# Stage ends split two chunks at a time, additions ahead of slab remainders, and a reordered start in a two-block float32 network on one core

## Chip, cores and metric

The kernel runs on one core of one Trainium2 chip. The metric is the time of one execution in microseconds (us), the median over runs.

## What is computed

Two residual blocks over one sequence of 256 tokens and 1024 channels, all in float32. Each has two layers. What matters here is that every sublayer begins with an RMS norm and a projection of the normalised input, and ends with an addition to x:

```python
def first_block(x, ...):
    for layer in range(2):
        h = rms_norm(x, norm_mix[layer])
        x = x + hybrid_mixer(h, w_in[layer], ...)
        h = rms_norm(x, norm_ffn[layer])
        x = x + (swiglu(h, ...) if layer == 0 else moe_swiglu(h, ...))   # 8 experts, top 2
    return rms_norm(x, final_norm)

def second_block(x, ...):
    for l in range(2):
        h = swiglu_ffn(rmsnorm(x, ffn1_pre_g[l]), ...)
        x = x + 0.5 * rmsnorm(h, ffn1_post_g[l])
        h = mixing_sublayer(rmsnorm(x, mix_pre_g[l]), ...)   # gMLP, pool, sparse attention, convolution
        x = x + rmsnorm(h, mix_post_g[l])
        h = swiglu_ffn(rmsnorm(x, ffn2_pre_g[l]), ...)
        x = x + 0.5 * rmsnorm(h, ffn2_post_g[l])
    return x
```

In `mixing_sublayer` the convolution branch starts with `a * sigmoid(gt)`, the gated input; the sparse attention keeps the 64 best of each row of scores.

## The kernel before

**Weights come as slabs.** All large weights are one stream of slabs of 128 x 2048 floats (1 MB). SyncE loads each in two halves into one of six places (`Sync.slabs`, line 276 on; DMAs at line 286). Since float32 products are built from rounded parts, each slab is split: ScalarE copies each half to the rounded part `whi` (`Scalar.hi`, line 326; three places), VectorE subtracts to get the remainder `wlo` (`Vector.lo`, line 823). TensorE then takes three matmuls of 128 x 512 per chunk of 128 input channels (`term`, lines 1485 to 1487): whi with XH, wlo with XH, whi with XL. A slab is 24 matmuls. A place of `whi` is free again when TensorE has finished its slab (the semaphore `pe_slab`).

**Activations are split the same way.** X holds the residual as two tiles (t = 0, 1) of 128 tokens x 1024 channels. At the entry of a sublayer TensorE transposes a tile in eight chunks of 128 x 128 into PSUM (`norm_tile`, line 1552), ScalarE copies them to XH with the gain applied (`split_tile`, line 348), VectorE makes XL (`rest_tile`, line 853). The RMS factor comes later (`norm_in`: two squares at line 369, a square root at line 371, a reciprocal on VectorE at line 874) and is applied to the results.

**Every order is written out by hand,** one program per engine; each engine works its instructions in that order and waits at semaphores in front of them. There are ten such entries: m0.n, f0n, m1.n, e.n in the first block (two mixers, an FFN, the experts) and g10n, x0m.n, g20n, g11n, x1m.n, g21n in the second. `ENTRY` names for each what makes the tile ready, the first PSUM bank of tile 0 and of tile 1 (four chunks fill a bank, so a tile takes two banks), and the point in the matmuls at which tile 1 is transposed.

**A stage end.** The last two slabs of a sublayer are worked as a pair (`leave`, through `pair`), tile 0 with both slabs before tile 1; in the middle of the last quarter TensorE transposes tile 0 of the next sublayer. The next two slabs are a pair again (`enter`): tile 0 with both, then tile 1 with both. In the entries with a 4 tile 1 is transposed ahead of the second slab's first half, with an 8 ahead of the third quarter. The wide mixers of the second block (x0m, x1m) start with a slab of 256-column matmuls in which tile 0 needs all eight chunks at once. The waits of TensorE in `pair` are for both halves of `wlo` (`dve_lo`) and, once per quarter, for half of XL or all of it:

```python
if split:
    pe.wait_ge(*k.at(f"{split}.l{t}{1 if half == KT else s}"))
for i, term in enumerate(terms[t * half:(t + 1) * half]):
```

On VectorE `rest_tiles` is the same place: it finishes tile 0 of the sublayer before, makes XL of tile 0, then the `wlo` that is still owed (`self.owed`, one slab), then finishes tile 1 (`add`, line 882, or `post`, lines 1279 to 1286), then XL of tile 1. On ScalarE `norm_in` first loads the sqrt table by a dummy root (`root_table`, line 354) at the first four entries, then copies tile 0, one slab, tile 1.

**The start.** SyncE loads X in four DMAs, then slabs. GpSimd loads the per-channel columns (`pcols`), makes the identity, and loads constants of the first mixer (`mload`, `mask_load`: 768 and 448 KB) and the router's weights. ScalarE and VectorE split two slabs (`LEAD`) before the first entry.

**The lower bounds.** In the first block's mixers VectorE builds 16 diagonal tiles after the entry (`lower_bounds`, line 906), on which TensorE waits ahead of line 1581.

**Wide mixers on VectorE** (`Vector.mixer2`): index scores (SCO, lines 1373 and 1375), a slab's `wlo`, the gated input (line 1379, waits for group z3 of the projection), a top-k in eight rounds (line 1329 on; it needs the scores after GpSimd's selects, line 2122), 31 convolution taps (line 1349). TensorE transposes the gated input (line 1975) after two more slabs.

**The final norm of the first block** follows the experts. Behind them each engine reads a flag and branches past a second pass over the experts that is only taken when one overflows.

## Time and profile before

| | |
|---|---|
| runs (us) | 2960.80, 2957.74, 2963.33 |
| median | 2960.80 |
| the profiled execution | 2955.16, its span 2953.4 |
| mean granted TensorE clock | 0.986 of full |
| TensorE busy | 2833.4 us (96%) |
| VectorE busy | 2061.2 us (70%) |
| ScalarE busy | 1706.6 us (58%) |
| bytes moved | 633.65 MB, mean 215 GB/s |

Times in rows of the timeline count from the start of the span. A row has start, duration, engine, line, operation, out<-in with shapes, how many instructions it merges, and in brackets how long the engine was idle before and what ended that. PE is TensorE's matmuls, PEld its weight loads, DVE VectorE, ACT ScalarE, POOL GpSimd, SP SyncE. Matmuls are pipelined, so a matmul's duration is longer than the distance to the next one's start. "issue" means that the profile shows nothing that the engine waited for.

### The profile page before, as it was taken

The page shows a single profiled execution, that of the slowest core. Times are in us where ns is not written, and L with a number is a line of the kernel's source. Part 1 is how long each engine was busy: PE and PEld are TensorE (multiplying, and loading weights), DVE is VectorE, ACT ScalarE, POOL GpSimd, SP SyncE. Part 2 cuts the span into 40 slices and gives each one's busy share as a digit, 9 for nine tenths or more (in the row PEclk, how much of TensorE's full clock was granted, in tenths as well). Part 3 has the DMA queues.
Part 4 walks back from the last instruction along what each step waited for, and adds up shares of the span by engine and source line. Part 5 has one row for each costly group of instructions (what it writes and reads, how often), then busy time and mean ns, then how long its engine had stood idle before and what let it go on. Part 6 is the DMA issues. An engine that isn't in the chain of part 4 may idle for free.

```text
span 2953.4 us, 34430 instructions
## 1 busy us (share of the span) xinstructions
PE 2833.4 (96%) x13288; PEld 2340.7 (79%) x13288; DVE 2061.2 (70%) x2999; ACT 1706.6 (58%) x2373; POOL 32.6 (1%) x55
## 2 busy tenths in 40 slices
PE   7999999999998999999999989999899999888999
PEld 5888888788876888888888868777778788776787
DVE  5577655657767989888988955587665554787554
ACT  5555554555565777777777754455454544554543
POOL 0000000000001000000000000000000000000000
PEclk9999999999998999999999999999999999999999
DMA  6444455453356999999999955554455555444453
GB/s 217 157 134 135 160 194 186 161 171 129 129 194 225 362 354 356 347 346 359 351 344 352 358 179 185 179 171 143 145 187 183 190 185 187 163 151 148 164 185 114
DMA packets 173979, 633.65 MB, mean 215 GB/s; under 512 B 19584, under 2 KB 19584, under 8 KB 173808
## 3 DMA queue, kind: packets, MB, share of 16 engines
q1 hardware_dynamic: 171072, 621.88, 60.9%
q0 software_dynamic: 2736, 9.49, 0.9%
q8 instruction: 107, 1.75, 0.2%
q14 instruction: 64, 0.52, 0.1%
HBM read 629.20 MB, written 2.10 MB: 214 GB/s over the span
## 4 chain that ended last, share of the span: by engine, by line
PE 86%; DVE 8%; ACT 3%; issue 1%; DMA 1%; SPq 0%; DVEq 0%; ACTq 0%
PE ps L1485 26%; PE ps L1487 26%; PE ps L1486 26%; DVE wlo L823 3%; PE ps L1655 2%; DVE CA L1349 2%; PE ps L1739 1%; PE ps L1790 1%; ACT whi L326 1%; DVE XL L853 1%; DMA raw<-in_W 1%; ACT XH L348 1%; PE ps L1641 1%; PE ps L1642 1%; PE ps L1542 0%
## 5 line engine op out<-in xcount | busy, mean ns | idle before, releaser
L823 DVE TENSOR_TENSOR wlo<-raw,whi 128x1024 fp32r<-128x1024 f32 x1182 | 1386.0, 1221 | 453.5 <-ACT whi L326 447.0
L326 ACT ACTIVATE whi<-raw 128x1024 fp32r<-128x1024 f32 x1182 | 1187.9, 1058 | 495.9 <-PE ps L1487 488.1
L1485 PE MATMUL ps<-whi,XH 128*128 128x512 f32 (+1 forms) x2064 | 821.6, 398 | 52.6 <-DVE XL L853 39.7
L1487 PE MATMUL ps<-whi,XL 128*128 128x512 f32 (+1 forms) x2064 | 806.8, 391 | 0.0
L1486 PE MATMUL ps<-wlo,XH 128*128 128x512 f32 (+1 forms) x2064 | 806.8, 391 | 0.0
L1485 PEld LDWEIGHTS ps<-whi,XH 128*128 128x128 f32 x2064 | 392.3, 190 | 141.9 <-issue 24.6
L1487 PEld LDWEIGHTS ps<-whi,XL 128*128 128x128 f32 x2064 | 391.9, 190 | 82.4
L1486 PEld LDWEIGHTS ps<-wlo,XH 128*128 128x128 f32 x2064 | 392.7, 190 | 76.8 <-issue 0.5
L1485 PE MATMUL ps<-whi,XEH 128*128 128x512 f32 x704 | 280.9, 399 | 3.1 <-DVE wlo L823 1.7
L1487 PE MATMUL ps<-whi,XEL 128*128 128x512 f32 x704 | 275.2, 391 | 0.0
L1486 PE MATMUL ps<-wlo,XEH 128*128 128x512 f32 x704 | 274.1, 389 | 0.0
L1485 PE MATMUL ps<-whi,GH 128*128 128x512 f32 x440 | 172.6, 392 | 0.0
L1486 PE MATMUL ps<-wlo,GH 128*128 128x512 f32 x440 | 171.3, 389 | 0.0
L1487 PE MATMUL ps<-whi,GL 128*128 128x512 f32 x440 | 171.3, 389 | 0.0
L1485 PEld LDWEIGHTS ps<-whi,XEH 128*128 128x128 f32 x704 | 132.2, 188 | 30.0 <-issue 2.3
L1487 PEld LDWEIGHTS ps<-whi,XEL 128*128 128x128 f32 x704 | 132.1, 188 | 28.8
L1486 PEld LDWEIGHTS ps<-wlo,XEH 128*128 128x128 f32 x704 | 132.5, 188 | 25.8
L555 ACT ACTIVATE GH<-ps 128x512 fp32r<-128x512 f32 x55 | 33.0, 599 | 206.9 <-PE ps L1739 206.9
L1090 DVE TENSOR_TENSOR GL<-ps,GH 128x512 fp32r<-128x512 f32 x55 | 38.0, 692 | 162.3 <-ACT GH L555 162.3
L1485 PE MATMUL ps<-whi,GH_ 128*128 128x512 f32 x352 | 144.2, 410 | 0.0
L1487 PE MATMUL ps<-whi,GL_ 128*128 128x512 f32 x352 | 137.4, 390 | 0.0
L1486 PE MATMUL ps<-wlo,GH_ 128*128 128x512 f32 x352 | 137.3, 390 | 0.0
(365 smaller groups left out, 2648.4 us busy)
## 6 DMA issues: line engine op xcount, KB each, us to landing
raw<-in_W SPq DMA_DIRECT2D x1182, 512.0 KB, 4.9
GP<-in_ffn_post_g POOLq DMA_DIRECT2D x4, 512.0 KB, 4.0
X<-in_x SPq DMA_DIRECT2D x4, 256.0 KB, 3.9
skew<-RB POOLq DMA_DIRECT2D x4, 256.0 KB, 6.0
RB<-skew POOLq DMA_DIRECT2D x8, 128.0 KB, 6.6
GP<-in_mix_post_g POOLq DMA_DIRECT2D x2, 512.0 KB, 3.8
out<-X SPq DMA_DIRECT2D x2, 512.0 KB, 2.6
mload<-in_cum_sums POOLq DMA_DIRECT2D x1, 768.0 KB, 9.3
```

Source lines behind the costliest of these rows:

```text
L326: act.activation(k.whi[:, slot, part], k.raw[:, at, part], ACT.Copy).then_inc(*k.up("act_hi"))
L348: x = act.activation(k.XH[:, 4 * h + c, t * P:(t + 1) * P], k.ps[:, bank + h, c * P:(c + 1) * P], ACT.Copy, scale=gain(4 * h + c))
L555: act.activation(GH[:, 2 * g:2 * g + 2, :], src, ACT.Copy).then_inc(*k.up("act_split", f"{T}.gh{g}"))
L823: dve.tensor_tensor(k.wlo[:, at, part], k.raw[:, at, part], k.whi[:, slot, part], ALU.subtract).then_inc(*k.up("dve_lo"))
L853: x = dve.scalar_tensor_tensor(out=k.XL[:, j, t * P:(t + 1) * P], in0=k.ps[:, bank + h, c * P:(c + 1) * P], scalar=gain(j), in1=k.XH[:, j, ...
L1090: dve.tensor_tensor(GL[:, 2 * g:2 * g + 2, :], src, GH[:, 2 * g:2 * g + 2, :], ALU.subtract).then_inc(*k.up("dve_split", f"{T}.gl{g}"))
L1349: x = dve.scalar_tensor_tensor(out=CA[:, c, :], in0=HP[:, c, j:j + S], scalar=dw(c, j), in1=CA[:, c, :], op0=ALU.mult, op1=ALU.add)
L1485: pe.matmul(ps, xh, k.whi[:, slot, cols], start=first, stop=False)
L1486: pe.matmul(ps, xh, k.wlo[:, at, cols], start=False, stop=False)
L1487: return pe.matmul(ps, xl, k.whi[:, slot, cols], start=False, stop=last)
L1641: pe.matmul(k.ps[:, 4 + 2 * t + half, :], k.LFH[:, b, t, :], cols, start=True, stop=False)
L1655: mm = pe.matmul(o, x, x, start=True, stop=True)
```

## The change

- A tile's eight chunks go to four PSUM banks, two in each. `ENTRY` lists the banks of both tiles. TensorE signals every two chunks (`norm_tile`), ScalarE and VectorE wait and signal every two (`split_tile`, `rest_tile`), and TensorE waits for XL ahead of every second term in `pair`, in the router ahead of every second chunk. Tile 1's transposes wait for the last XL of tile 0.
- At f0n, m1.n and e.n VectorE finishes tile 1 (two additions) before the owed `wlo`, not after it.
- The dummy root at m0.n moves to the start of ScalarE's program. At f0n and m1.n it goes, so that the table load falls to the square root of line 371. At e.n it moves ahead of the last slab copy of the mixer before.
- Start: SyncE issues tile 0 of X, slab 0, tile 1, slab 1, and the rest. ScalarE and VectorE split one slab before the first entry, VectorE owes the next. GpSimd's constants wait until six half slabs have been copied.
- In the wide mixers VectorE's gated input moves up ahead of one slab's `wlo` and the scores.
- Final norm: ScalarE's first square waits for tile 0's last scatter addition, not for tile 1's.

```diff
-ENTRY = {"m0.n": ("x", 2, 6, 4), "f0n": ("m0.out", 4, 6, 4), "m1.n": ("f0.out", 2, 6, 4), "e.n": ("m1.out", 4, 6, 0), "g10n": ("fin.out", 2, 6, 8),
-         "x0m.n": ("g10p.out", 2, 6, 8), "g20n": ("x0m.p.out", 2, 4, 8), "g11n": ("g20p.out", 2, 6, 8),
-         "x1m.n": ("g11p.out", 2, 6, 8), "g21n": ("x1m.p.out", 2, 4, 8)}
+UP, OVER = (2, 3, 6, 7), (4, 5, 6, 7)
+ENTRY = {"m0.n": ("x", UP, UP, 4), "f0n": ("m0.out", OVER, OVER, 4), "m1.n": ("f0.out", UP, UP, 4), "e.n": ("m1.out", OVER, (4, 5, 0, 2), 0),
+         "g10n": ("fin.out", (0, 1, 2, 3), UP, 8), "x0m.n": ("g10p.out", UP, (3, 6, 7, 4), 8), "g20n": ("x0m.p.out", (0, 1, 2, 3), (2, 3, 4, 5), 8),
+         "g11n": ("g20p.out", UP, UP, 8), "x1m.n": ("g11p.out", UP, (3, 6, 7, 4), 8), "g21n": ("x1m.p.out", (0, 1, 2, 3), (2, 3, 4, 5), 8)}
...
                 sp.dma_start(k.X[:, t, part], k.a["x"][t * P:(t + 1) * P, part]).then_inc(*k.up(f"d_x{t}{h}", f"x{t}{h}", 16))
+            self.slabs(t + 1)
...
-        bank = ENTRY[tag][1 + t]
-        for h in range(2):
-            act.wait_ge(*k.at(f"{tag}.tp{t}{h}"))
-            for c in range(4):
...
+        banks = ENTRY[tag][1 + t]
+        for p in range(KT // 2):
+            act.wait_ge(*k.at(f"{tag}.tp{t}{p}"))
+            for c in (2 * p, 2 * p + 1):
+                x = act.activation(k.XH[:, c, t * P:(t + 1) * P], k.ps[:, banks[p], c % 2 * P:(c % 2 + 1) * P], ACT.Copy, scale=gain(c))
+            x.then_inc(*k.up("act_split", f"{tag}.h{t}{p}"))
...
-        if tag in ("m0.n", "f0n", "m1.n", "e.n"):
-            self.root_table()
         self.split_tile(tag, 0, gain)
...
-        self.early = 1
+        self.early = 0 if tag == "m0.n" else 1
...
-        self.hi(4)
+        self.hi(3)
+        if l:
+            self.root_table()
+        self.hi()
...
-        act.wait_ge(*k.at("x.end_dve"))
-        for t in range(NT):
+        for t in range(NT):
+            act.wait_ge(*k.at("x.end_dve" if t else "x.end_dve0"))
...
         act.wait_ge(*k.at("ones1"))
-        self.hi(LEAD)
+        self.root_table()
+        self.hi()
...
         self.rest_tile(tag, 0, gain)
+        added = tag in ("f0n", "m1.n", "e.n")
+        if added:
+            self.finish(1)
         self.lo(self.owed)
         self.owed = 0
-        if self.finish:
+        if self.finish and not added:
             self.finish(1)
...
         self.lo()
+        dve.wait_ge(*k.at(T + "z3"))
+        dve.tensor_tensor(A, A, GT, ALU.mult).then_inc(*k.up("dve_gate", T + "h"))
         self.lo()
         dve.wait_ge(*k.at(T + "rel"))
...
         self.lo()
-        dve.wait_ge(*k.at(T + "z3"))
-        dve.tensor_tensor(A, A, GT, ALU.mult).then_inc(*k.up("dve_gate", T + "h"))
...
-        self.lo(LEAD)
+        self.lo()
+        self.owed = 1
...
-                if split:
-                    pe.wait_ge(*k.at(f"{split}.l{t}{1 if half == KT else s}"))
                 for i, term in enumerate(terms[t * half:(t + 1) * half]):
                     if between and i:
                         between(8 * t + 4 * s + 4 * i / half)
+                    if split and i % 2 == 0:
+                        pe.wait_ge(*k.at(f"{split}.l{t}{i // 2 if half == KT else 2 * s + i // 2}"))
...
+        for p in range(KT // 2):
+            if p % 2 == 0:
+                pe.wait_ge(*k.at(f"{ready}{t}{p // 2}"))
+            if t and p == 0:
+                pe.wait_ge(*k.at(f"{tag}.l03"))
...
+        pool.wait_ge(k.of("act_hi"), 2 * RING)
         pool.dma_start(k.mload[:], k.a["cum_sums"]).then_inc(*k.up("d_mload", "mload", 16))
```

The order of instructions at three places. First ScalarE at the start, before (ACTIVATE whi is half a slab, XH one chunk, `small` the dummy root, later the RMS square root):

```order
L326 ACT_TABLE_LOAD
L326 ACTIVATE whi<-raw 128x1024 x4
L354 ACT_TABLE_LOAD
L354 ACTIVATE small<-small 128x1
L348 ACTIVATE XH<-ps,pcols 128x128 x8
L326 ACTIVATE whi<-raw 128x1024 x2
L348 ACTIVATE XH<-ps,pcols 128x128 x8
L369 ACTIVATE XN,small<-X 128x1024 x2
```

and now:

```order
L356 ACT_TABLE_LOAD
L356 ACTIVATE small<-small 128x1
L328 ACTIVATE whi<-raw 128x1024 x2
L350 ACTIVATE XH<-ps,pcols 128x128 x8
L328 ACTIVATE whi<-raw 128x1024 x2
L350 ACTIVATE XH<-ps,pcols 128x128 x8
L369 ACTIVATE XN,small<-X 128x1024 x2
L371 ACTIVATE small<-small 128x2
```

One slab's two halves stand ahead of the first XH instead of two slabs', and the table load of the root stands ahead of everything.

VectorE at f0n, before (XL one chunk, `wlo` half a slab, X<-ps an addition of 512 columns):

```order
L882 TENSOR_TENSOR X<-ps,X 128x512 x2
L853 SCALAR_TENSOR_TENSOR XL<-ps,pcols,XH 128x128 x8
L823 TENSOR_TENSOR wlo<-raw,whi 128x1024 x2
L882 TENSOR_TENSOR X<-ps,X 128x512 x2
L853 SCALAR_TENSOR_TENSOR XL<-ps,pcols,XH 128x128 x8
L874 RECIPROCAL small<-small 128x2
```

and now:

```order
L888 TENSOR_TENSOR X<-ps,X 128x512 x2
L856 SCALAR_TENSOR_TENSOR XL<-ps,pcols,XH 128x128 x8
L888 TENSOR_TENSOR X<-ps,X 128x512 x2
L827 TENSOR_TENSOR wlo<-raw,whi 128x1024 x2
L856 SCALAR_TENSOR_TENSOR XL<-ps,pcols,XH 128x128 x8
L880 RECIPROCAL small<-small 128x2
```

The additions of tile 1 and the owed half slabs have changed places; m1.n and e.n read alike.

VectorE in a wide mixer, before (Z<-Z is the gated input, SCO the index scores, WRK the top-k's copy):

```order
L1366 TENSOR_SCALAR small<-small 128x8
L823 TENSOR_TENSOR wlo<-raw,whi 128x1024 x4
L1373 TENSOR_SCALAR SCO<-XN,small 128x256 x2
L1375 SCALAR_TENSOR_TENSOR SCO<-XN,small,SCO 128x256 x6
L823 TENSOR_TENSOR wlo<-raw,whi 128x1024 x2
L1379 TENSOR_TENSOR Z<-Z 128x2x256
L1380 MEMSET HP 128x2x30
L1329 COPY WRK<-SCO 128x512
```

and now:

```order
L1373 TENSOR_SCALAR small<-small 128x8
L827 TENSOR_TENSOR wlo<-raw,whi 128x1024 x2
L1376 TENSOR_TENSOR Z<-Z 128x2x256
L827 TENSOR_TENSOR wlo<-raw,whi 128x1024 x2
L1382 TENSOR_SCALAR SCO<-XN,small 128x256 x2
L1384 SCALAR_TENSOR_TENSOR SCO<-XN,small,SCO 128x256 x6
L827 TENSOR_TENSOR wlo<-raw,whi 128x1024 x2
L1387 MEMSET HP 128x2x30
```

The gated input has moved ahead of two half slabs and of the eight score instructions.

## Rows read from the trace of the kernel before

**Rows 1.** The page: busy us, share of the span, instructions of each engine.
```profile
PE 2833.4 (96%) x13288; PEld 2340.7 (79%) x13288; DVE 2061.2 (70%) x2999; ACT 1706.6 (58%) x2373; POOL 32.6 (1%) x55
```
**Rows 2.** What TensorE waited for: us in total, times, longest.
```profile
PE ps L1485 <- DVE XL L853: 39.7, 15, 13.9
...
PE ps L1975 <- DVE Z L1379: 5.7, 2, 2.9
```
**Rows 3.** Timeline of TensorE at three entries: x0m.n (twice) and g21n.
```profile
1910.16 0.35 PE L1485 MATMUL ps<-whi,XH 128*128 128x256 f32 x1 [1.79 <-DVE XL L853]
...
1919.88 0.38 PE L1485 MATMUL ps<-whi,XH 128*128 128x256 f32 x1 [2.99 <-DVE XL L853]
...
2766.41 0.50 PE L1485 MATMUL ps<-whi,XH 128*128 128x512 f32 x1 [1.96 <-DVE XL L853]
```
**Rows 4.** Timeline of the start.
```profile
12.84 1.06 ACT L326 ACTIVATE whi<-raw 128x1024 fp32r<-128x1024 f32 x1 [0.78 <-DMA raw<-in_W]
...
21.44 0.76 PE L1485 MATMUL ps<-whi,XH 128*128 128x512 f32 x1 [13.91 <-DVE XL L853]
```
**Rows 5.** Windows of the start: stretch, length, busy us (count), PEclk, DMA share, GB/s.
```profile
0.00:5.00 5.00, 0.00 (x0) 0.00 (x0) 0.22 (x2) 0.00 (x0) 3.46 (x11) 1.00 0.59 184
5.00:8.00 3.00, 1.97 (x8) 1.57 (x8) 0.00 (x0) 0.00 (x0) 0.73 (x3) 1.00 1.00 245
8.00:21.00 13.00, 0.00 (x0) 0.00 (x0) 5.74 (x8) 8.89 (x15) 0.00 (x0) 1.00 1.02 399
```
**Rows 6.** Timeline of the stage end f0n.
```profile
354.26 1.28 ACT L354 ACT_TABLE_LOAD   x1
...
355.19 0.39 PE L1486 MATMUL ps<-wlo,CVH 128*128 128x512 f32 x1
355.42 0.39 PE L1487 MATMUL ps<-whi,CVL 128*128 128x512 f32 x1
...
355.67 2.17 ACT L348 ACTIVATE XH<-ps,pcols 128x128 fp32r<-128x128 f32 x8
356.83 2.16 DVE L853 SCALAR_TENSOR_TENSOR XL<-ps,pcols,XH 128x128 fp32r<-128x128 f32 x8 [6.03 <-ACT XH L348]
...
358.10 0.47 PE L1485 MATMUL ps<-whi,XH 128*128 128x512 f32 x1 [2.29 <-DVE XL L853]
...
358.91 2.35 DVE L823 TENSOR_TENSOR wlo<-raw,whi 128x1024 fp32r<-128x1024 f32 x2
...
361.18 1.28 DVE L882 TENSOR_TENSOR X<-ps,X 128x512 f32<-128x512 f32 x2
...
362.52 1.03 PE L1552 MATMUL ps<-ident,X 128*128 128x128 f32 x8
```
**Rows 7.** Timeline behind the experts, ScalarE and VectorE.
```profile
1708.60 1.28 ACT L354 ACT_TABLE_LOAD   x1 [4.89 <-issue]
...
1713.06 0.16 DVE L1263 RECIPROCAL small<-small 128x1 f32<-128x1 f32 x1 [4.39 <-ACT small L647]
```
**Rows 8.** Timeline of the first wide mixer, VectorE and GpSimd.
```profile
1937.64 2.36 DVE L823 TENSOR_TENSOR wlo<-raw,whi 128x1024 fp32r<-128x1024 f32 x2 [7.32 <-ACT whi L326]
...
1943.43 2.70 POOL L2122 TENSOR_SCALAR_AFFINE_SELECT SCO<-SCO 128x256 f32<-128x256 f32 x2 [27.46 <-DVE SCO L1375]
...
1946.78 0.43 DVE L1329 COPY WRK<-SCO 128x512 f32<-128x512 f32 x1
...
1963.51 2.36 DVE L823 TENSOR_TENSOR wlo<-raw,whi 128x1024 fp32r<-128x1024 f32 x2 [0.95 <-ACT whi L326]
```
**Rows 9.** Windows behind four waits, columns as in rows 5.
```profile
358.80:362.20 3.40, 3.40 (x10) 2.65 (x9) 3.40 (x5) 0.92 (x1) 0.00 (x0) 0.50 0.41 167
884.50:894.60 10.10, 4.71 (x22) 3.44 (x23) 6.46 (x16) 6.71 (x16) 0.54 (x1) 0.50 0.33 125
1919.90:1923.30 3.40, 3.40 (x26) 3.33 (x27) 2.20 (x3) 1.38 (x4) 0.00 (x0) 1.00 0.00 0
2522.80:2526.20 3.40, 3.40 (x19) 3.40 (x18) 3.33 (x6) 1.37 (x2) 0.00 (x0) 0.50 0.61 222
```

More of the change, by code:

```diff
@@ L847, in rest_tile @@
         dve, k = self.eng, self.k
-        bank = ENTRY[tag][1 + t]
-        for h in range(2):
-            dve.wait_ge(*k.at(f"{tag}.h{t}{h}"))
-            for c in range(4):
-                j = 4 * h + c
-                x = dve.scalar_tensor_tensor(out=k.XL[:, j, t * P:(t + 1) * P], in0=k.ps[:, bank + h, c * P:(c + 1) * P], scalar=gain(j),
-                                             in1=k.XH[:, j, t * P:(t + 1) * P], op0=ALU.mult, op1=ALU.subtract)
-            x.then_inc(*k.up("dve_split", f"{tag}.l{t}{h}"))
+        banks = ENTRY[tag][1 + t]
+        for p in range(KT // 2):
+            dve.wait_ge(*k.at(f"{tag}.h{t}{p}"))
+            for c in (2 * p, 2 * p + 1):
+                x = dve.scalar_tensor_tensor(out=k.XL[:, c, t * P:(t + 1) * P], in0=k.ps[:, banks[p], c % 2 * P:(c % 2 + 1) * P], scalar=gain(c),
+                                             in1=k.XH[:, c, t * P:(t + 1) * P], op0=ALU.mult, op1=ALU.subtract)
+            x.then_inc(*k.up("dve_split", f"{tag}.l{t}{p}"))
     def rest_tiles(self, tag, gain):
@@ L1166, in experts @@
             self.scatter(T, NE - 1, t)
+        k.events[f"{T}.end_dve0"] = k.events[f"{T}.add{NE - 1}.0"]
         k.events[f"{T}.end_dve"] = k.events[f"{T}.add{NE - 1}.1"]
@@ L1547, in norm_tile @@
         pe, k = self.eng, self.k
-        ready, bank = ENTRY[tag][0], ENTRY[tag][1 + t]
-        for h in range(2):
-            pe.wait_ge(*k.at(f"{ready}{t}{h}"))
-            for c in range(4):
-                mm = pe.transpose(k.ps[:, bank + h, c * P:(c + 1) * P], k.X[:, t, (4 * h + c) * P:(4 * h + c + 1) * P], k.ident[:])
-            mm.then_inc(*k.up("pe_turn", f"{tag}.tp{t}{h}"))
+        ready, banks = ENTRY[tag][0], ENTRY[tag][1 + t]
+        for p in range(KT // 2):
+            if p % 2 == 0:
+                pe.wait_ge(*k.at(f"{ready}{t}{p // 2}"))
+            if t and p == 0:
+                pe.wait_ge(*k.at(f"{tag}.l03"))
+            for c in (2 * p, 2 * p + 1):
+                mm = pe.transpose(k.ps[:, banks[p], c % 2 * P:(c % 2 + 1) * P], k.X[:, t, c * P:(c + 1) * P], k.ident[:])
+            mm.then_inc(*k.up("pe_turn", f"{tag}.tp{t}{p}"))
     def enter(self, tag, first, second, events):
```

12 lines of the change are left out of this document (5 added, 7 removed).

## The prediction

> **What bounds the kernel now.** I read the page first: TensorE is busy for 96% of the span [rows 1], so outside a few places nothing else can be worth time, and the 120 us in which it is idle are all there is to win, with what its clock loses. Next comes the list of what TensorE waits for: the remainders XL of the normalised input (line 853), 39.7 us in 15 waits, and the gated input Z (line 1379), 5.7 us in 2 [rows 2]. Then the timeline of one stage end, step by step [rows 6], and of the start [rows 4], to see which engine holds TensorE there; the other ends repeat the pattern [rows 3]. What the reader is to see is that at a stage end three engines work in a row: TensorE transposes, ScalarE copies (XH), VectorE subtracts (XL), and TensorE stands still until the first piece has gone through all three. The size of that piece is what the change halves or quarters.
>
> **Pieces and pace.** Eight transposes take 1.03 us, so 0.13 each; eight copies 2.17, so 0.27 each; eight remainders 2.16, so 0.27 each [rows 6]. A piece of four chunks becomes one of two: a wait that contains the whole chain shrinks by two of each, 0.26 + 0.54 + 0.54 = 1.34 us. Later pieces need not be feared: six matmuls of 512 columns follow per pair of chunks (0.23 us each from start to start, 355.19 to 355.42 [rows 6]), 1.36 us, against 0.54 for the next pair on ScalarE and VectorE.
>
> **1. Start.** TensorE begins at 21.44, after 13.91 us of idleness, and the second half of the first slab has landed only at 12.84 [rows 4]. Bytes moved: 184 GB/s for 5 us, 245 for 3, then 399 [rows 5]; at 12.84 that is 3.6 MB (an estimate), though input and first slab are 2.1 MB: the constants (1.25 MB) were in between. Now pcols, half the input and the slab come first, 1.62 MB, which the same rates have moved at 7.9; the second half of the input and the second slab are then there at 11.9. The sqrt table is loaded while nothing waits for it. Working on: copy of the half slab 1.06 to 9.0, its remainder 1.2 to 10.2, two XL 0.6, start at 10.9. The second slab's remainder (behind XL on VectorE, copies of 1.06 each behind XH on ScalarE) ends near 14.9; TensorE has then done four chunks of the first slab and eight transposes if it runs at full clock (14.7), and is not yet there (16) at the lower one, which its first matmul had (0.76 against 0.39). Gain about **10.8**. The first lower-bound chain starts as much earlier. ScalarE now has two slabs to copy behind it instead of one, 2 us; what hides them is that it waits for TensorE itself a little later, and without that cover the third group of matmuls would come up to 2 us later. The constants start with the sixth copied half slab near 23 and are needed after the first six groups, near 100 us: nothing. Bounds: if later slabs share the bandwidth with the first, it may land near 10.3 (gain 8.4); at most 12.
>
> **2. Second token tile, where it was waited for in full.** At the four FFN entries of the second block the wait is 1.96 [rows 3] (the last of four alike) and becomes 0.6: 4 x 1.34 = 5.4, less 0.05 each for two more signals: 5.2. At the two wide mixers the first matmuls wait for all eight chunks, 2.99 [rows 3]; now two fewer copies, six fewer remainders and two fewer transposes stand in the way: 0.54 + 1.62 + 0.26 = 2.42 each; I take 4.7. Together **9.9**.
>
> **3. First token tile of the second block.** The copies end 1.1 us sooner for the first pair, but the second slab's remainder is queued on VectorE behind all eight XL, and TensorE needs it after four chunks. That is the wait that comes next. The XL end only some 0.5 earlier. At the three FFN entries behind a mixer or an FFN this leaves 0.45 each. At the wide mixers idle is 1.79 [rows 3]; TensorE then does 24 short matmuls (3.0 us) while the remainder takes 2.35, so 0.8 were in hand and the gain is 0.5 + 0.8 = 1.25 each. At the first entry of the second block nothing is owed, but VectorE finishes tile 1 first; between 0.45 and 1.1 I take 0.7. Together **4.5**.
>
> **4. f0n and m1.n.** The pair before ends at 355.81; the table load keeps XH back to 355.67, and the matmuls start at 358.10 [rows 6]. Without the load (1.28 and 0.15 around it) XH starts at 354.3, XL at 354.9, and the first two are there at 355.6: no wait. Then the next waiting: four chunks to 358.6, the additions (now straight after XL, 357.2 to 358.5) let the transposes run to 359.6, and the remainder moved behind the additions ends at 358.5 + 2.35 = 360.8. TensorE waits 1.2 us and goes on at 360.9; before, it got there at 363.3, after a stretch in which matmuls took 0.63 from start to end. Gain 2.4. The load isn't gone: it now comes before the Sqrt (line 371). In f0n TensorE covers it. In m1.n it stands in the chain to the lower bounds, on which TensorE also waits, but the chain starts earlier by that same load and by the additions: again 2.4. Together **4.8**. The Trainium skill (ScalarE: Activation LUTs, section What ACT_TABLE_LOAD costs) states some 1.38 us of drain beside a load of 1.28; here the first copy follows 0.13 us after the load's end, with the dummy root in between [rows 6], so the trace doesn't agree. By the skill's figure m1.n would gain 1.0 and the sum be 1.4 less.
>
> **5. e.n.** Here the load is issued earlier, in an idle stretch, and tile 1 can't be turned before its addition, which stood behind the load (1.43) and the slab remainder (2.35) [rows 6]. Both go from its way: **3.8**. The router behind it is a chain of small steps and moves as a whole.
>
> **6. Gated input in the wide mixers.** TensorE waits 2.85 us twice. VectorE's product now goes into its idle time of 7.32 [rows 8]: ScalarE finishes group z3 ahead of the copies for which VectorE is idle there. So the wait goes. But from there to the channel sum VectorE is the limit, and TensorE merely arrives sooner at its next waits for remainders. What counts is how much sooner VectorE is: not by the whole product, since its next step waits for GpSimd, whose two selects end at 1943.43 + 2.70 = 1946.13 against 1946.78 [rows 8]: 0.6; and in the first mixer its waits for copied slabs fall too, 0.95 at 1963.51 [rows 8] and a smaller one before it, together 1.5. **2.7** in all for both. Bounds: 1.2 (no such wait falls) and 5.7 (both waits of TensorE go in full).
>
> **7. Final norm.** Split flags let the first square start before the second addition. ScalarE's table load begins at 1708.60 with nothing to wait for but the branch before it, and VectorE's reciprocal at 1713.06, long after its input [rows 7]. The branch sets both: **0**.
>
> **8. Clock.** Behind some of these waits the granted clock is 0.50, that is 1.2 of 2.4 GHz: 3.4 us at 358.8, and again in the second wide mixer at 2522.8 [rows 9]. At half the clock such a stretch does the work of 1.7 us, so it costs up to 1.7. In 4 this is contained. For the entry of the second wide mixer I add **1.4**, short of 1.7 because a wait lay in it as well.
>
> **Sum.** 10.8 + 9.9 + 4.5 + 4.8 + 3.8 + 2.7 + 0 + 1.4 = 37.9 us, against the profiled execution's 2955.2 (span 2953.4): 2917.3. That execution stands 5.6 below the median of the runs shown, 2960.8, so for a median I forecast **2922.9**. What a measurement here can tell from no change is 0.2%, 5.9 us.
>
> **Rivals.** *The clock doesn't follow* (0.12). What stays is not nothing: 1.2 at f0n and m1.n, 0.6 at six waits for tile 1. For it: 2.29 us of idleness before 358.10 led to a slow stretch [rows 6, 9], and 1.2 is not far below. Against it: behind 2.99 at 1919.88 [rows 3] the clock stayed full [rows 9]. Then 4.2 of the gains in 4 and 8 fall away, and four ends that had no stretch get one, 6.8: gain 27, **2934**. *The slabs aren't sooner* (0.10): if the first slab lands at 12.84 as before, because bandwidth and not order holds it, TensorE starts at 15.8, gain 5.6 in place of 10.8: **2928**. Against it: 3.6 MB had been moved by then. *More comes back* (0.05): slow stretches of 10 us at e.n [rows 9] and at the first entry of the second block shorten by a third each and the mixers' upper bound holds: gain 44, **2917**. *Slower* (0.03): where TensorE was stopped once it now may be stopped four times, from bank to bank, and each stop may keep the clock low. At e.n the trace shows what this costs: 0.50 for 10.1 us [rows 9], 5.1 lost. Two more such stretches at each of ten ends are 101 us, less 38: **3024**; from 3.8 us lost per end on the change is no gain. Against it: while a pair's next pieces come in 0.54 and are used in 1.36 no stops arise. The Trainium skill has such a case (TensorE: Matmul & The Clock Gate, section A second HAM failure mode: psum-queue depth-cycling): short idle times while going round the banks make the clock swing. By that rule this rival would come true; no row here shows stops of that kind. *Nothing measurable* (0.02): gains at the ends and the start each swallowed by an unseen wait, 2960.
>
> **Numbers.** The forecast has 0.68. Lower gain: start -2.4, clock -4.2, mixers -1.5, so 30; upper 43 (start +1.2, mixers +3, and one slow stretch less). With 2.5 us for the spread of the runs shown this is 2915 to 2934, and the first rival's time, itself uncertain by 1, takes it to 2935; outside lie the slow rival and no change, 0.05, and the tails of the others. Faster 0.95 (all but the last two), same 0.02, slower 0.03.
>
> **What would show it.** Right: TensorE's first 512-column matmul near 11 (wrong if after 14); waits for XL down from 39.7 to about 5 us beyond the start's share, new ones for the slab remainder (line 827) of 1.2 at f0n and m1.n; no wait for line 1376, but longer ones for remainders and for the channel sum before 2011; 1708.60 and the table load there merely shifted. Wrong: ten or more waits per end; slow stretches behind each; VectorE idle between the top-k and the channel sum.

## The result, and the profile after

| | before | changed |
|---|---|---|
| median of the runs | 2959.27 (2956.76 to 2963.33, 4 runs) | 2924.86 (2917.68 to 2925.10, 4 runs) |
| ratio | | 0.9876, 95% interval 0.9861 to 0.989 |
| the profiled execution, its span, granted clock | 2955.16, 2953.4, 0.986 | 2924.62, 2922.9, 0.988 |
| the changed kernel once more, as a control (e9) | 2959.04 (7 runs) | 2916.91 (2916.17 to 2917.00, 4 runs), ratio 0.9856 (0.984 to 0.9873); span 2915.1, granted clock 0.990 |

The change is faster, by 34.4 us in one measurement and 42.1 in the other; the forecast was 37.9. The same program was measured at two times 8 us apart; e9 below shows where they differ. A "slow stretch" is one in which the granted clock is recorded as 0.50 [rows 9]. The page after, to be read against [rows 1]:

```profile
PE 2835.2 (97%) x13288; PEld 2341.1 (80%) x13288; DVE 2060.9 (71%) x2999; ACT 1702.8 (58%) x2370; POOL 36.9 (1%) x55
```

TensorE's busy time hasn't fallen, although no matmul was added and 30.5 us went: what fell is its idle time, from 120.0 to 87.7. What it waited for after, in us, times and longest:

```profile
PE ps L1493 <- DVE wlo L827: 17.1, 17, 2.0
PE ps L1550 <- DVE XN L1447: 13.9, 2, 6.9
PE ps L1493 <- DVE XL L856: 8.8, 8, 3.8
PE ps L1563 <- DMA pcols<-in_pcols: 7.5, 1, 7.5
PE ps L1928 <- DVE CA L1356: 5.7, 2, 2.8
PE ps L1563 <- DVE X L1275: 5.4, 1, 5.4
```

The remainders XL fell from 39.7 in 15 waits [rows 2] to 8.8 in 8, 3.8 of it at the start, so 5.0 elsewhere, as forecast; the wait for Z is gone. Slab remainders (wlo) are now the largest item. Where the time went shows best as distances between the same events in three traces, beside the sum of the prediction's terms for each stretch. "Tile 1 at" an entry is the first matmul of the second token tile there; the channel sum is L1928 (L1917 before):

| stretch, from the event above to | before | changed | changed, e9 | forecast gain | gain, gain e9 |
|---|---|---|---|---|---|
| lower bounds of the first mixer | 36.70 | 29.98 | 29.64 | 10.8 (term 1) | 6.7, 7.1 |
| lower bounds of the second (f0n, m1.n between) | 528.05 | 520.47 | 520.47 | 4.8 (4) | 7.6, 7.6 |
| the router's sums, L1884 (e.n between) | 334.55 | 332.18 | 330.50 | 3.8 (5) | 2.4, 4.1 |
| tile 1 at g10n | 828.33 | 827.03 | 827.15 | 2.0 (2, 3) | 1.3, 1.2 |
| tile 1 at x0m.n | 192.25 | 189.14 | 189.10 | 3.6 (2, 3) | 3.1, 3.2 |
| channel sum of the first wide mixer | 91.84 | 89.80 | 89.81 | 2.1 (6) | 2.0, 2.0 |
| tile 1 at g20n | 137.46 | 139.37 | 137.19 | 1.8 (2, 3) | -1.9, 0.3 |
| tile 1 at g11n | 190.54 | 189.15 | 189.12 | 1.8 (2, 3) | 1.4, 1.4 |
| tile 1 at x1m.n | 193.75 | 189.10 | 189.14 | 5.0 (2, 3, 8) | 4.7, 4.6 |
| channel sum of the second wide mixer | 91.67 | 89.84 | 89.82 | 0.6 (6) | 1.8, 1.9 |
| tile 1 at g21n | 141.27 | 139.47 | 135.80 | 1.8 (2, 3) | 1.8, 5.5 |
| end of the span | 186.99 | 187.37 | 187.36 | 0 | -0.4, -0.4 |
| sum | 2953.4 | 2922.9 | 2915.1 | 38 | 30.5, 38.3 |

**The start after.** Rows of ScalarE, VectorE and TensorE, then windows with the columns of [rows 5]:

```profile
9.05 1.06 ACT L328 ACTIVATE whi<-raw 128x1024 fp32r<-128x1024 f32 x1 [6.75 <-DMA raw<-in_W]
10.29 1.06 ACT L328 ACTIVATE whi<-raw 128x1024 fp32r<-128x1024 f32 x1 [0.19 <-DMA raw<-in_W]
...
10.14 2.47 DVE L827 TENSOR_TENSOR wlo<-raw,whi 128x1024 fp32r<-128x1024 f32 x2 [9.03 <-ACT whi L328]
12.53 2.15 DVE L856 SCALAR_TENSOR_TENSOR XL<-ps,pcols,XH 128x128 fp32r<-128x128 f32 x8
...
13.28 0.77 PE L1493 MATMUL ps<-whi,XH 128*128 128x512 f32 x1 [3.80 <-DVE XL L856]
...
18.54 1.23 PE L1563 MATMUL ps<-ident,X 128*128 128x128 f32 x8
```

```profile
0.00:5.00 5.00, 0.00 (x0) 0.00 (x0) 0.22 (x2) 1.49 (x2) 1.38 (x7) 1.00 0.51 142
5.00:8.00 3.00, 0.49 (x3) 0.49 (x4) 0.00 (x0) 0.00 (x0) 0.00 (x0) 1.00 0.91 291
...
13.30:18.50 5.20, 5.20 (x12) 3.99 (x13) 3.65 (x8) 2.00 (x3) 0.00 (x0) 1.00 1.03 418
```

The slab's second half is there at 10.29, not at 7.9. By 8.0 the queues had moved 142 x 5 + 291 x 3, so 1.6 MB, as much as everything up to the slab's end holds; but it wasn't those 1.6 MB alone: from 2.67 on SyncE had issued the transfers behind them, and by 10.29 2.38 MB had moved. The bound written down was landing 10.3, gain 8.4; this trace has 10.29 and, for the first matmul, 8.2 (21.44 to 13.28). How exactly that fits is partly luck. Eight traces have this start unedited (the changed kernel, e3, e4, e5, e7, e9, e10, e12), and in them ScalarE's copy of the second half begins at 9.20 to 10.29, the first matmul at 12.18 (e3) to 13.28, the first lower bounds at 28.50 to 29.98. Against the one trace of before the gain is thus 8.2 to 9.3 at the first matmul and 6.7 to 8.2 at the lower bounds. In this trace another 1.2 goes to TensorE's pace: all twelve matmuls ahead of the transposes (13.28 to 18.54) follow each other by some 0.43, in the kernel before only the first six, and then by 0.23; in the other seven it is seven to twelve.

**f0n after**, VectorE and TensorE, in place of [rows 6]:

```profile
346.35 2.16 DVE L856 SCALAR_TENSOR_TENSOR XL<-ps,pcols,XH 128x128 fp32r<-128x128 f32 x8 [3.98 <-ACT XH L350]
348.43 1.28 DVE L888 TENSOR_TENSOR X<-ps,X 128x512 f32<-128x512 f32 x2
349.62 2.35 DVE L827 TENSOR_TENSOR wlo<-raw,whi 128x1024 fp32r<-128x1024 f32 x2
...
349.96 1.03 PE L1563 MATMUL ps<-ident,X 128*128 128x128 f32 x8
352.03 0.50 PE L1493 MATMUL ps<-whi,XH 128*128 128x512 f32 x1 [1.03 <-DVE wlo L827]
```

As forecast: no wait for XL, tile 1 turned without one, and a new wait of 1.03 (1.2 expected) for the slab remainder behind the additions.

### The profile page after: what moved, and what is told of

It is laid out like the page before. It is cut to its first block, busy times and chain, and to the rows that moved or that the text cites. A ratio compares the mean times of both kernels' runs of the same rounds, so it can differ in the third digit from the quotient of the medians.

```text
span 2922.9 us, 34438 instructions
## 1 busy us (share of the span) xinstructions
PE 2835.2 (97%) x13288; PEld 2341.1 (80%) x13288; DVE 2060.9 (71%) x2999; ACT 1702.8 (58%) x2370; POOL 36.9 (1%) x55
## 4 chain that ended last, share of the span: by engine, by line
PE 86%; DVE 9%; ACT 3%; issue 1%; DMA 1%; POOL 0%; SPq 0%; DVEq 0%; ACTq 0%; POOLq 0%
PE ps L1493 26%; PE ps L1495 26%; PE ps L1494 26%; DVE wlo L827 3%; PE ps L1666 2%; DVE CA L1356 2%; PE ps L1750 1%; PE ps L1801 1%; ACT whi L328 1%; DVE XL L856 1%; DMA raw<-in_W 1%; PE ps L1652 1%; PE ps L1653 1%; PE ps L1550 0%; DVE Z L1443 0%
```

## Experiments

Twelve kernels ran, e1 to e8 on one chip and e9 to e12 on another, each with runs of the kernel before beside it. Their medians are compared with the control's 2916.9, since those runs agree within 1 us; the medians of before beside the three sets of runs are 2958.7, 2961.8 and 2959.0, so a difference below about 3 is read from the trace and not from the medians.

**e1, pieces of four chunks.** The table ENTRY and the loops of split_tile, rest_tile, norm_tile, pair and the router's waits as before, everything else changed:

```diff
-        for p in range(KT // 2):
-            act.wait_ge(*k.at(f"{tag}.tp{t}{p}"))
-            for c in (2 * p, 2 * p + 1):
+        for h in range(2):
+            act.wait_ge(*k.at(f"{tag}.tp{t}{h}"))
+            for c in range(4):
```

> The changed kernel with pieces of four chunks again at the stage ends (banks, copies, remainders, transposes and their signals as before); start, order of the additions, table load, gated input and final norm stay changed. Theory (the pieces carry about half the gain): tile-1 waits of the second block back from 0.70 to 1.96 four times and to 2.99 twice, 9.6 us; the first tile there 4.5; f0n and m1.n 0.75 each; start 1.1; clock 1.4: 18 us slower than the change, 2943. Rival 1 (the gain is in the order of the additions and the start, the pieces only fill time that the slab remainder sets anyway): tile 1 alone, 9.6: 2934.5. Rival 2 (going round four banks costs clock): no slower than the change, 2925 or less.

Measured: 2941.18 (2936.24 to 2948.04), 24 slower than the control. In its trace the waits for XL are back:

```profile
PE ps L1493 <- DVE XL L856: 26.8, 15, 4.0
```

From the last experts' scatter on, the six entries are 0.9, 3.1, 2.1, 1.4, 4.6 and 1.6 longer than in e9, 13.8 in all before rounding (14.1 plus 1.4 of clock expected); f0n and m1.n cost 1.7 once the clock is counted out (1.5 expected). Another 3 us are slow stretches in the second wide mixer. Theory held, both rivals fell: the pieces carry about half the gain, and if going round four banks costs anything, it is less than they bring (the two were not separated).

**e2, the start of before.**

```diff
-            self.slabs(t + 1)
...
-        self.root_table()
-        self.hi()
+        self.hi(LEAD)
...
-        pool.wait_ge(k.of("act_hi"), 2 * RING)
```

> The changed kernel with the start of before: all input and then slabs, mixer constants at once, two slabs copied ahead of the first stage end, table load there. Theory (from the trace after: first 512-column matmul 13.28 against 21.44, of which the smaller pieces give 1.1): first matmul at about 20.3, and 7 us slower, 2932. Rival 1 (the forecast's price, 10.8 less 1.1): 2934.6. Rival 2 (the first lower-bound chain swallows most of an earlier start): the shift seen at the first slab gone by the end of the first mixer's groups, under 3 us slower, 2927.

Measured: 2923.25, 6.3 slower than the control; first matmul at 21.24 and the first lower bounds at 37.59 against 29.64 to 29.98 in the two traces of the changed kernel, 7.6 to 8.0 later. The whole shift survives the first mixer (f0n's second slab 7.6 later). In the whole span 2.3 of it are made up by places that weren't edited, 1.4 of them behind the first channel sum, where e9 has a slow stretch and e2 none. The theory held but for its 20.3. The first matmul comes 0.2 sooner than before although the slab's second half landed 0.7 later (13.53 against 12.84): from the first copy of the input to the matmul it is 1.40 in place of 2.43, so the pieces bring their 1.0.

**e6 and e11, the parts of the start.** One kernel loads the constants at once, the other issues the whole input before the first slab:

```diff
-        pool.wait_ge(k.of("act_hi"), 2 * RING)
```

> The changed kernel with the mixer constants and masks loaded at once instead of behind the sixth copied half slab; the order of input and slabs stays changed. Theory (1.25 MB more share the bandwidth before the first slab is complete): first 512-column matmul 2 to 3 us later than 13.28, near 15.7. Rival (the order of SyncE's transfers did it, the constants run beside them): first matmul within 0.7 of 13.28.

```diff
-            self.slabs(t + 1)
```

> The changed kernel with all four pieces of the input ahead of the first slab on SyncE, constants still late and one slab copied ahead of the stage end. Theory (the gain at the start is that one slab and not two is copied and subtracted before the first piece of the input, 2.1 and 2.4 us, and that half the input is 0.5 MB less in front): first 512-column matmul 1 to 1.5 later than 13.3, near 14.5. Rival (the order of transfers is the whole gain): near 17 or later.

Measured: 2915.98 and 2917.97. TensorE's first matmul in e6:

```profile
13.07 0.77 PE L1493 MATMUL ps<-whi,XH 128*128 128x512 f32 x1 [3.35 <-DVE XL L856]
19.86 0.50 PE L1493 MATMUL ps<-whi,XH 128*128 128x512 f32 x1 [1.01 <-DVE wlo L827]
```

It is at 13.07 there, at 13.32 in e11, at 12.18 to 13.28 with the changed start. Neither edit alone shows beyond that scatter (e6's second slab is late by a wait of 1.01, which the next wait, for the lower bounds, takes up), so the constants theory (15.7) fell and e11's (14.5) too. Only in e2, where both are undone, does the second half land at 13.53 in place of 9.20 to 10.29. What is left is the rest of the chain: with two slabs ahead the input's copies follow at 19.84, behind the second slab (to 18.42) and a table load of 1.28.

**e3, additions behind the slab remainder.**

```diff
-        added = tag in ("f0n", "m1.n", "e.n")
+        added = False
```

> The changed kernel with tile 1's addition behind the owed slab remainder on VectorE at f0n, m1.n and e.n, as before. Theory: e.n 2.35 later; at f0n and m1.n the wait for the remainder (1.0) goes but the transposes of tile 1 wait for the additions 2.25 instead, 1.2 later each: 4.8 us slower, 2929.7. Rival (at f0n and m1.n the two orders trade one wait for an equal one): 2.4 slower, 2927.3, with the difference at e.n alone.

Measured: 2917.95, 1.0 slower. At f0n the wait moves from the slab remainder (1.03) to the transposes (1.32), and from tile 0's first transpose to the matmul behind tile 1's transposes it is 7.48 in place of 7.06, so 0.4; at m1.n the same, and the lower bounds behind it wait 2.98 in place of 1.83. At e.n:

```profile
869.37 2.35 DVE L827 TENSOR_TENSOR wlo<-raw,whi 128x1024 fp32r<-128x1024 f32 x2
871.64 1.28 DVE L888 TENSOR_TENSOR X<-ps,X 128x512 f32<-128x512 f32 x2
873.77 2.16 DVE L856 SCALAR_TENSOR_TENSOR XL<-ps,pcols,XH 128x128 fp32r<-128x128 f32 x8 [0.84 <-ACT XH L350]
```

and in the changed kernel:

```profile
868.54 2.16 DVE L856 SCALAR_TENSOR_TENSOR XL<-ps,pcols,XH 128x128 fp32r<-128x128 f32 x8 [3.98 <-ACT XH L350]
870.61 1.28 DVE L888 TENSOR_TENSOR X<-ps,X 128x512 f32<-128x512 f32 x2
871.81 2.35 DVE L827 TENSOR_TENSOR wlo<-raw,whi 128x1024 fp32r<-128x1024 f32 x2
874.07 2.16 DVE L856 SCALAR_TENSOR_TENSOR XL<-ps,pcols,XH 128x128 fp32r<-128x128 f32 x8
...
871.35 1.47 PE L1563 MATMUL ps<-ident,X 128*128 128x128 f32 x8 [1.79 <-DVE X L888]
874.83 0.37 PE L1873 MATMUL ps<-XH,RWS 128*16 128x256 f32 x1 [2.01 <-DVE XL L856]
```

The same work of VectorE stands between the two XL in either order. From the first XL to the second it is 6.47 in e3 and 5.53 in the changed kernel: 0.9, and not 2.35; from the end of the pair before (869.17 + 0.39 in the changed kernel) to the router's sums (L1884) 13.59 against 13.07 and 13.12, 0.5. The total of some 2.4 (0.4 at f0n, 1.5 at m1.n with its lower bounds, 0.5 at e.n) is the rival's, but for another reason: most of it is at m1.n, not at e.n. The medians alone, 1.0 apart, can't tell this.

**e4, the table ahead of the copies.**

```diff
+        if tag in ("f0n", "m1.n", "e.n"):
+            self.root_table()
         self.split_tile(tag, 0, gain)
...
-        self.hi(3)
-        if l:
-            self.root_table()
-        self.hi()
+        self.hi(4)
```

> The changed kernel with the sqrt table loaded ahead of the copies at f0n, m1.n and e.n, as before. Theory (a load costs 1.28 and 0.15 around it, no drain): XH 1.4 later at each, TensorE's first wait at f0n and m1.n 1.2 later at each, e.n 1.4: 3.8 us slower, 2928.7. Rival 1 (each load drains the engine for 1.38 more before the next copy): XH 2.8 later at each, 7.5 slower, 2932.4. Rival 2 (in m1.n the load stands in the chain to the lower bounds in either place, at f0n the remainder sets the wait anyway): e.n alone, 1.4 slower, 2926.3.

Measured: 2918.78, 1.9 slower. f0n in e4, ScalarE and TensorE:

```profile
346.65 1.28 ACT L356 ACT_TABLE_LOAD   x1
347.95 0.20 ACT L356 ACTIVATE small<-small 128x1 f32<-128x1 f32 x1
348.06 2.16 ACT L350 ACTIVATE XH<-ps,pcols 128x128 fp32r<-128x128 f32 x8
...
349.45 0.47 PE L1492 MATMUL ps<-whi,XH 128*128 128x512 f32 x1 [1.25 <-DVE XL L855]
```

The added wait is 1.25 at f0n and 1.23 at m1.n (1.2 each expected), and by the distance used in e3 each costs 1.5 (8.59 against 7.06); but at m1.n the lower bounds, with the load no longer in their chain, then wait 0.55 in place of 1.83: 1.3 is given back. At e.n it is 14.36 from the pair's end to the router's sums in place of 13.1, 1.3 more. Together about 3.0, between the theory and rival 2. Rival 1 fell: from the end of the load to the first copy it is 0.13, with the root in between.

**e5, the gated input behind again.**

```diff
-        dve.wait_ge(*k.at(T + "z3"))
-        dve.tensor_tensor(A, A, GT, ALU.mult).then_inc(*k.up("dve_gate", T + "h"))
         self.lo()
         dve.wait_ge(*k.at(T + "rel"))
...
         self.lo()
+        dve.wait_ge(*k.at(T + "z3"))
+        dve.tensor_tensor(A, A, GT, ALU.mult).then_inc(*k.up("dve_gate", T + "h"))
         dve.memset(HP[:, :, 0:30], 0.0)
```

> The changed kernel with the product for the gated input behind the scores and a slab remainder again, in both wide mixers, as before. Theory (VectorE is the limit up to the channel sum): TensorE waits 2.85 for Z twice, its waits for remainders before the channel sum are shorter, and from the first matmul of tile 1 to the channel sum the stretch is 91.8 in the first and 91.7 in the second mixer, as before, in place of 89.8: 3.9 us slower in these two stretches. Rival 1 (the forecast's terms): 2.1 in the first, 0.6 in the second. Rival 2 (each wait of 2.85 counts in full): 5.7. The time of the whole is this plus or minus 7, which slow stretches of TensorE's clock add or take: 2922 to 2929.

Measured: 2918.76 (2915.74 to 2922.09), 1.9 slower. From tile 1 to the channel sum 90.60 and 90.35, against 89.80 and 89.84: 1.3 in both mixers together, below all three expectations, although both waits of 2.84 for Z are back. So the moved product alone isn't what shortened 91.84 to 89.80. The rest is in the clock behind the wait for Z, and in what VectorE then waits for. In the kernel before, first mixer:

```profile
1946.00:1952.80 6.80, 6.07 (x17) 4.92 (x18) 6.59 (x17) 2.49 (x3) 0.14 (x1) 0.50 0.31 114
1956.92 2.36 DVE L823 TENSOR_TENSOR wlo<-raw,whi 128x1024 fp32r<-128x1024 f32 x2 [0.62 <-ACT whi L326]
```

and in e5, first mixer (a window, a row) and second (a window):

```profile
1926.30:1929.70 3.40, 3.40 (x10) 2.62 (x9) 3.26 (x13) 2.30 (x3) 0.00 (x0) 0.50 0.21 87
1940.95 2.36 DVE L827 TENSOR_TENSOR wlo<-raw,whi 128x1024 fp32r<-128x1024 f32 x2 [0.28 <-ACT whi L328]
2532.20:2539.00 6.80, 6.78 (x32) 5.70 (x33) 6.59 (x18) 3.11 (x4) 0.00 (x0) 1.00 0.27 100
```

The releasers in the traces read thus: a slow stretch behind the wait for Z delays TensorE's slab, ScalarE's next copy waits for that slab, and VectorE for the copy. With 6.8 us of it VectorE waits 0.62 and 0.95 [rows 8], with 3.4 us 0.28, with none not at all, and the distances are 91.84, 90.60 and 90.35. The second mixer of before has none there either; its 91.67 is 90.35 and a slow stretch at 2533.0, just as tile 1 begins, which costs 1.3 (VectorE's first wait for a copied slab ends 6.93 behind tile 1's first matmul, 5.61 in the first mixer). So the move itself is worth 0.5 in each mixer (90.35 to 89.82), and the rest of 91.84 and 91.67 is the clock's, not the pieces'. The wait for Z comes with such a stretch in two of its four cases (before and e5, first mixer each).

**e7 and e10, a shift.** Eight or sixteen more transposes ahead of those of g10n, into a bank that the real ones overwrite, and nothing else:

```diff
+            if tag == "g10n" and t == p == 0:
+                for _ in range(8):
+                    pe.transpose(k.ps[:, banks[0], 0:P], k.X[:, 0, 0:P], k.ident[:])
```

> The changed kernel with eight more transposes (1.03 us of TensorE, their result overwritten) ahead of the first at g10n, and nothing else. Theory (which waits in the wide mixers are followed by a slow stretch depends on when they fall, not on what the change did there): the stretches behind 1988 and 2063 and their two fellows in the second mixer come or go although nothing there was edited; the time is 1.03 longer plus or minus 1.7 for each stretch, 2918 to 2926, and not 2925.9. Rival (the longer waits that the earlier product leaves before the channel sum cause them): the same stretches, each 1.0 later, and 2925.9.

> The changed kernel with sixteen more transposes (2.06 us of TensorE) ahead of the first at g10n. Theory (stretches depend on when waits fall): the time doesn't follow the shift; between 2916 and 2927, with another set of slow stretches behind 1695 than with eight. Rival (only the first small shift cured something): one more us than with eight, 2918.3, and the same stretches.

Measured: 2917.30 (2916.63 to 2917.67, 5 runs) with eight, 2918.31 (2917.23 to 2923.72) with sixteen. The kernel with more work is 7.5 faster than the first measurement of the changed kernel. In the second wide mixer, which isn't touched, the changed kernel (first trace) has these stretches behind the channel sum and behind the wait for XL at L1434:

```profile
2596.00:2599.40 3.40, 3.34 (x11) 2.88 (x12) 3.33 (x6) 0.00 (x0) 0.00 (x0) 0.50 0.48 192
2671.10:2674.50 3.40, 3.40 (x10) 2.62 (x9) 2.83 (x3) 1.39 (x2) 0.00 (x0) 0.50 0.00 0
```

and e7, at the same events:

```profile
2592.40:2595.80 3.40, 3.39 (x19) 2.98 (x20) 3.37 (x5) 1.47 (x4) 0.00 (x0) 1.00 0.83 295
2667.50:2670.90 3.40, 3.40 (x17) 2.82 (x16) 1.82 (x3) 0.58 (x1) 0.00 (x0) 1.00 0.00 0
```

At the lower level (0.50, 1.2 of 2.4 GHz) TensorE starts 10 and 11 instructions in 3.4 us, at the full one 17 and 19. With sixteen neither is there either, and the stretch behind the first mixer's channel sum, which with eight still stands at 1987.9, is gone too. e7's rival fell. That of e10 had the time right (2918.3) and only the stretches wrong. The theory isn't shown by this: the unedited program differs from its first measurement in the same way (e9), so these two runs can't tell what a shift does from what comes and goes by itself.

**e9, the control.** No edit.

> The changed kernel itself, unedited, as a control beside the others. Theory (its time is the sum of its waits plus slow stretches that come or go from run to run and with small shifts): runs fall into a group near 2917 and one near 2925, with granted clocks of 0.991 and 0.987. Rival (the slow stretches belong to this schedule, which has the additions ahead, the table late and the earlier product all at once): all runs within 1.5 of 2925.

Measured: 2916.91, all four runs within 0.9, clocks 0.990 to 0.991. So the theory's two groups don't lie within this set but between it and the first (2924.62, 2925.10 and 2925.10 at 0.987 and 0.988, and 2917.68 at 0.991); the rival fell. The chip may differ between the two sets; one run of the first set at the other time says that it isn't needed. The second wide mixer in the first trace:

```profile
2587.49 0.50 PE L1493 MATMUL ps<-whi,XH 128*128 128x512 f32 x1 [1.98 <-DVE wlo L827]
2596.06 2.08 PE L1928 MATMUL ps<-CA,ones 128*128 128x256 f32 x4 [2.83 <-DVE CA L1356]
...
2669.82 0.50 PE L1493 MATMUL ps<-whi,XH 128*128 128x512 f32 x1 [1.93 <-DVE XL L1434]
```

and in e9:

```profile
2583.38 0.50 PE L1493 MATMUL ps<-whi,XH 128*128 128x512 f32 x1 [1.96 <-DVE wlo L827]
2591.94 1.13 PE L1928 MATMUL ps<-CA,ones 128*128 128x256 f32 x4 [1.22 <-DVE CA L1356]
...
2664.09 0.50 PE L1493 MATMUL ps<-whi,XH 128*128 128x512 f32 x1 [1.93 <-DVE XL L1434]
```

One program, and it reads thus. The channel sum comes 8.57 and 8.56 behind the wait before it in both, because VectorE sets it. In e9 a slow stretch (2584.4 to 2587.8) lies inside that time and costs nothing: TensorE merely arrives later and waits 1.22 in place of 2.83. In the first trace the stretch lies behind the channel sum, where TensorE is the limit: four matmuls take 2.08 in place of 1.13, and it is 73.76 to L1434 in place of 72.15; behind L1434 another 1.7 go the same way. In all fourteen traces the distance from a channel sum to L1434 is either 72.1 to 72.2 or 73.7 to 73.8, whatever was edited: 73.7 or more in eight of 28 cases, all behind a channel sum that TensorE waited 2.81 to 2.83 for, and 72.1 to 72.2 in the eighteen behind a wait of some 1.2 (and in two, in e3 and e8, behind 2.8). Of the 7.8 between the two spans 3.7 are behind this channel sum, 2.2 behind the first mixer's, 1.7 behind the second lower bounds and 0.3 at the start (table above). What starts a slow stretch in one execution and not in the other stays open.

**e12, the final norm's flags together.**

```diff
-        for t in range(NT):
-            act.wait_ge(*k.at("x.end_dve" if t else "x.end_dve0"))
+        act.wait_ge(*k.at("x.end_dve"))
+        for t in range(NT):
```

> The changed kernel with the final norm's first square behind both additions again. Theory (the branch before it sets the start): from the last scatter's first matmul to the first transpose of g10n 8.86 as in the changed kernel, with 0.3 either way. Rival (the square comes one addition sooner): 0.7 longer, 9.5.

Measured: 2915.33 (2912.17 to 2916.70), not slower; from the scatter to the transposes 9.70, but the other kernels, whose norm is the changed one, spread from 8.71 to 9.97 here. Not told apart, and worth nothing in the time.

**e8, a version that goes further.**

```diff
-                    pe.wait_ge(k.of("dve_lo"), 2 * (self.n - 2 + s) + 2)
+                    pe.wait_ge(k.of("dve_lo"), 2 * (self.n - 2 + s) + (1 if by_half else 2))
...
+                    if t == 0 and by_half and i == 2:
+                        pe.wait_ge(k.of("dve_lo"), 2 * (self.n - 2 + s) + 2)
```

In ENTRY the last number of the six entries of the second block is 7 in place of 8; at m0.n the first slab's copies and remainders stand between the second and third piece of the input's.

> The changed kernel with three additions. At the stage ends TensorE waits for the owed slab's remainder half by half (its first two chunks need the first half only); in the second block tile 1 is turned one chunk earlier; at the start the first slab's copies and remainders come between the first and second half of the input's. Theory: the waits for the remainder at f0n and m1.n (1.0 each) and the six of 0.6 in the second block go, 5.9; six waits of 0.70 for tile 1 go, 4.2; first matmul 1.5 to 2 sooner than 13.28: 12 us faster but for the clock, 2913 plus or minus 7. Rival (VectorE is as late with what comes next: the waits move behind, to tile 1's additions and copies): 3 us, 2922.

Measured: 2911.90 (2910.66 to 2917.16, 5 runs), ratio to before 0.983 (0.9816 to 0.9843), the fastest of all; 5.0 below the control's median. First matmul at 11.86 (11.3 to 11.8 expected; the changed start scatters from 12.18 to 13.28); the waits for slab remainders at the entries and for tile 1 are gone. But:

```profile
PE ps L1495 <- DVE wlo L828: 13.9, 10, 2.2
...
PE ps L1568 <- DVE X L1296: 3.5, 5, 0.8
```

Tile 1 is now waited for one step earlier, at its addition: 3.5 of the 4.2 come back. At m1.n the wait for the lower bounds grows from 1.83 to 2.98, so 1.1 comes back there too. The 5.0 lie between the rival's 3 and the theory's 12, for the rival's reason.

## Why the prediction was right, and where not

The direction and the mechanism were right, and the size was within the range: 37.9 us forecast, 30.5 and 38.3 in the two traces, 34.4 and 42.1 in the medians. That e9's 38.3 agrees so well with 37.9 is partly luck: terms 1 to 7 were forecast at 36.5 and come to some 32 (an estimate: 7, 12.4, 5.9, 4.1 and 2.6 from the items below), and slow stretches that the trace of before has and e9 hasn't make up the rest. By terms:

1. **Start, 10.8: mis-sized.** 8.2 at the first matmul, 6.7 to 7.1 at the lower bounds (9.3 and 8.2 in the best of the eight traces). The failed step is "which the same rates have moved at 7.9": the rates came true (1.6 MB by 8.0), but it gave the first slab the whole bandwidth. Of the sum only the bound named beside it (10.3) came. That "the constants were in between" as the cause is only half right: with either the constants' delay or the order alone the slab lands about as early (copied from 10.34 in e11, 10.09 in e6).
2. and 3. **Tile 1, 9.9, and tile 0, 4.5: right in kind, 2 us too large, and that in tile 0.** Tile 1's wait is 0.70 at all six entries (0.6 forecast), so 4 x 1.26 + 2 x 2.29 = 9.6 of 9.9; tile 0's next wait is for the slab remainder, 0.57 to 0.72. With slow stretches counted at half their length the six entries give 12.4 of 14.4, which leaves tile 0 some 2.8 of 4.5. e1 shows the same from the other side.
4. **f0n and m1.n, 4.8: 7.6 in the table,** of which 1.7 is a slow stretch at 37.9 in the trace of before. Neither trace of the changed kernel has one there, but e10, the same program up to g10n, has one at 30.1. That leaves 5.9: by the distance used in e3 2.85 at each entry (9.91 to 7.06; 2.4 forecast), and 0.2 at the lower bounds. The waits are as forecast. Taken back one at a time, the additions are worth 1.9 here (e3), the table 1.7 (e4), the pieces 1.7 (e1), together 5.3 of the 5.9. The table's is what is left of 3.1, since at m1.n the wait for the lower bounds gives 1.3 back.
5. **e.n, 3.8: right in sum, wrong in its parts.** From the end of the pair before to the router's sums it was 17.1 and is 13.1 in both traces, 4.1. (The table's 2.4 in the first trace has a slow stretch of 1.7 at the lower bounds in it, 551.4 to 554.8.) But "both go from its way" fails for the slab remainder: it moved from before the addition to before the next XL, and the router needs both tiles' XL. Alone the addition's place gives 0.5 (e3), the table 1.3 (e4), the pieces, which the term left out, 0.8 (e1: 13.89); the other 1.5 comes only with all three. Up to the first of the router's matmuls (L1873), with less of the slow stretches in it, it is 9.70 before and 5.27 in both traces of the changed kernel, and 6.20 (e3), 6.78 (e4) and 6.29 (e1): 0.9, 1.5 and 1.0 of 4.4, with 1.0 left. Where that comes from is not shown.
6. **Gated input, 2.7: 3.9 in the stretches, 1.3 by taking the move back (e5).** The parts are nearly the forecast's: 0.5 in each mixer for the product (0.6 forecast), and in the first VectorE's waits for copied slabs gone (0.62 and 0.95; 1.5 forecast). What the term didn't have is why those waits were there, a slow stretch behind the wait for Z, and the 1.3 of another at 2533.0 (e5). "TensorE merely arrives sooner at its next waits" was right: the waits before the channel sum are 7.7 in the first mixer before (2.85 for Z, 1.68, 1.98, 1.19) and 8.2 after (0.88, 1.96, 0.51, 1.99, 2.83).
7. **Final norm, 0: right.** The table load starts 3.51 behind the scatter, as before (3.52), with its 4.89 of "issue" ahead of it [rows 7].
8. **Clock, 1.4: right at x1m.n (4.7 in the table against 3.1 at x0m.n), wrong as the whole account.** The prediction reckoned with what the clock does at the places that change, not with stretches that come and go elsewhere. Behind the two channel sums they took some 3.5 each in the first trace (139.37 and 139.47, against 135.6 to 136.0 where none falls); in e9 they took 1.4 behind the first and none behind the second, where before has two (2625.2 and 2700.3).

The rivals: the clock did follow at f0n, and m1.n's stretch moved behind the lower bounds in the first trace only. The slow one did not come: no entry has more than two waits, and behind none of those of 0.57 to 1.03 does a slow stretch begin in these two traces. So the case of the Trainium skill in which short idle times while cycling through banks make the clock swing (TensorE: Matmul & The Clock Gate, section A second HAM failure mode: psum-queue depth-cycling) did not arise at these entries. The Trainium skill's drain of 1.38 us beside a table load (ScalarE: Activation LUTs, section What ACT_TABLE_LOAD costs) shows neither at f0n before nor in e4: from the load's end to the first copy it is 0.13 in both, and the measurement decides.

## What to carry to other kernels

Where three engines hand a piece on in a row, the idle time is the first piece's; halve it, but then reckon with what is queued on the same engine behind the pieces, for it becomes the next wait. Moving one work item past another on the same engine gains only if the engine that waits doesn't need both of them: write down the distance between the two ends that matter, as from XL to XL at e.n, and not the item's own length. And where slow stretches of the clock come and go, compare distances between equal events in two traces of the same program before crediting an edit with a few microseconds.
